# Eight written-out expert steps and a job table made on TensorE and ScalarE, in a four-layer transformer kernel

## The chip, the cores and the metric

The kernel runs on one core of one Trainium2 chip. The metric is the time of one execution on the device in microseconds, the median of three runs. The profile is of one further execution.

## The reference, cut to what matters

The program is two blocks of two layers each, over 256 tokens of width 1024. The first block has attention layers with dense feed-forward parts. Its second layer (layer 1 of the kernel) is a sparse attention whose input product also yields 48 gate columns, and which compresses keys and values with two small weights, `cmp_k_w1` and `cmp_v_w1`. The second block has two layers with a mixture of 32 experts, two experts for each token:

```
experts = grp[:, None] * EXPERTS_PER_GROUP + top_local          # 256 tokens x 2
def expert_block(args):
    xb, e = args
    return (jax.nn.silu(xb @ w_gate[e]) * (xb @ w_up[e])) @ w_down[e]
```

Each expert has a gate and an up weight of 1024x512 and a down weight of 512x1024, in float32: 6 MB for an expert. Which experts get tokens is known only when the router has run. An expert without tokens adds nothing to the output.

## The kernel before, in words

Everything is one program with an instruction stream written for each engine. SyncE (SP) issues nearly all weight loads, in the order in which they are written, each after a wait for the buffer that it overwrites.

**The expert stage.** There are two, one for each layer of the second block. A job is up to 64 slots (`W`) of one expert. After the router, TensorE counts the tokens of each expert. `wm` is the number of jobs of each expert, and expert 0 gets one at least. From these come three results in PSUM bank 3, which VectorE turns into the table `tab`: the expert of each job, the first slot of each job, and `more`, the number of loop rounds. VectorE writes `tab` with three small instructions (L2498, L2499, L2501) between the selection matrix `sel` of token tile 0 and that of tile 1. SP, TensorE, ScalarE and VectorE read registers from `tab`. TensorE runs three dummy products, `spin(3)` (L1673), between the table's products and the gather (L1723) that brings the tokens into slots.

Each job loads six pieces of 1 MB: two of gate, two of up, two of down. Job 0 is always expert 0, and its pieces are loaded before the table is there. TensorE's step `j` makes the gate and up products of job `j` (L1757), transposes (L1766, L1776), and the down products of job `j-1` (L1787). `used` counts the pieces that TensorE has done with.

**Where the pieces go.** `raw` has six places of 1 MB. `spare` has six more, which share their memory with `parts`, the split weights of the other stages. `FIXED` = 6 jobs are handled by code that is written out: jobs 0, 2 and 4 (`IN_PARTS`) go to `spare`, jobs 1, 3 and 5 to `raw`, so up to twelve pieces can be on the way or waiting. From job 6 on, all pieces go to the six places of `raw`. Steps 1 to 5 are written out, the steps after them are a loop over `more` rounds, and the last step and the end are written out again. In the loop the gate piece of the next job waits until TensorE has used the gate piece of this job in the same place. That is in `home_free`:

```
return at(j, 6, q - 7)
```

**Weights elsewhere.** In the other stages a weight is split: ScalarE rounds a piece to its high part (L801) and VectorE subtracts to get the low part (L1941), into one of three places of `parts` (`split_to`). TensorE's products use both parts.

**The gates of layer 1.** The last group of layer 1's input product has 48 columns (`n == 48`). TensorE makes it transposed, ScalarE copies it to `gate_t` (L854), TensorE turns it back (L1613), ScalarE and VectorE each write one token tile of the gates (L859, L1986), and then TensorE goes on with the position products (L1618). The products with the compression windows (L1608) come before and after that, first with `cmp_k_w1`, then with `cmp_v_w1`. Both engines split `cmp_v_w1` ahead of their part in the gates. ScalarE also squares the keys here, which VectorE sums for head norms (L1993).

Of the kernel before, what the change touches and what calls it, by code (L numbers as in the profile page):

```python
# [23 lines left out]
ALU = mybir.AluOpType  # L24
ACT = mybir.ActivationFunctionType
# [23 lines left out]
SPL = 3  # L49
HALF = 2048  # L50
JOBS = NE + NS // W
FIXED = 6
IN_PARTS = (0, 2, 4)
EPS = 1e-6
OFF = -1.0e30
BIG = 3.0e38
# [16 lines left out]
def build(nc, A, out):  # L73
    ctx = ExitStack()
    with ctx:
# [321 lines left out]
        def job_home(l, j, q):  # L397

            if isinstance(j, int) and j <= FIXED:
                job, i = piece(j, q)  # L400
                if job in IN_PARTS:
                    part = (SPL0[2 * l + 1] + i // 2) % SPL
                    return spare[:, 2 * part + i % 2, :], arrived[2 * l][i], 16 * (LOADS0[l][i] + job // 2 + 1)
                if job < FIXED - 1 or j < FIXED:
                    place = (RAW0[2 * l + 1] + i) % RAW
                    return raw[:, place, :], arrived[2 * l + 1][place], 16 * ((job + 1) // 2)
            place = (RAW0[2 * l + 1] + q - 2) % RAW
            return raw[:, place, :], arrived[2 * l + 1][place], at(j, 16, -48 if q < 2 else -32)

        def consumed(job, i):  # L410

# [4 lines left out]
        def home_free(j, q):  # L416

            if isinstance(j, int) and j <= FIXED:
                job, i = piece(j, q)
                if job in IN_PARTS or job == 3 or (job == 5 and i < 4):  # L420
                    return consumed(job - 2, i)
                if job == 5:
                    return consumed(5, i - 2)
                return consumed(3, 4 + i) if i < 2 else consumed(5, i - 2)
            return at(j, 6, q - 7)

        SHAPES = [(4, DE), (4, DE), (2, D)]
# [203 lines left out]
        def _(sp):  # L631
# [33 lines left out]
            for l in range(2):  # L665
                seg = 2 * l
                for i in range(len(stream[seg])):
                    if l == 0 and i == 2:
                        load_x(1, x2_loaded)
                    if l == 0 and i == RAW:  # L670
                        for dst, src in PARS[1:NPAR0] + [(cst[:, P:], A["consts"][:, P:]), (oneh, A["onehot"]), (tmask, A["row_masks"]), (relb[:], A["rel_bias"])]:
                            sp.dma_start(dst, src).then_inc(par_loaded, 16)
                    load(seg, i)
                def gate_up_of(j, e):
                    for q, m, hf in gate_up(j):
                        load_job(l, j, e, q, m, hf)

                def down_of(j, e, last=False):
                    for hf in range(2):
                        load_job(l, j, e, down_at(last) + hf, 2, hf)  # L680

                sp.wait_ge(lo_done[2 * l], len(stream[2 * l]))
                gate_up_of(0, 0)
                down_of(1, 0)
                sp.wait_ge(tab_done, l + 1)
                more = sp.value_load(tab[0:1, 2 * JOBS:2 * JOBS + 1], min_val=NS // W - FIXED - 1, max_val=JOBS - FIXED - 1)
                e = expert(1)
                gate_up_of(1, e)
                down_of(2, e)
                for j in range(2, FIXED + 1):  # L690
                    if j > 2:
                        before = e
                    e = expert(j)
                    gate_up_of(j, e)
                    if j > 2:
                        down_of(j, before)
                with sp.Fori(0, more) as j:
                    e, before = expert(at((j, 1), 1, 0)), expert(at((j, 1), 1, -1))
                    gate_up_of((j, 1), e)
                    down_of((j, 1), before)  # L700
                end = (more, 1)
                down_of(end, expert(at(end, 1, -1)), last=True)
# [82 lines left out]
        def _(act):  # L785
# [59 lines left out]
            def evac_proj(layer, hi):  # L845
                seg = SEG[layer]
                for g in range(PJ_AT[layer], hi):
                    pieces, n, dst = PJ[g]
                    if layer == 1 and g == PJ_AT[1] + 4:
                        compress_in()  # L850
                    split_to(seg, pieces[-1][0] + 3)
                    if n == 48:
                        act.wait_ge(used[seg], pieces[-1][0] + 1)
                        nc.scalar.activation(gate_t, pb[2][0:n, 0:S], ACT.Copy).then_inc(win_a, 1)  # L854
                    act.wait_ge(pj_ready, g + 1)
                    act.wait_ge(rstd_done, ROOT_AT[("norm", N_PROJ[layer])])
                    d = qkv_t(0)[:, dst:dst + n] if layer < 2 else qkv2[:, 0, dst:dst + n]
                    x = pb[2][:, S:S + n] if n == 48 else pb[(2 * g) % 4][:, 0:n]
                    nc.scalar.activation(d, x, ACT.Copy, scale=rstd(N_PROJ[layer], 0)).then_inc(pj_a, 1)  # L859
                    if layer < 2 and g - PJ_AT[layer] in HEADS_AT[layer]:  # L860
                        if layer and g == PJ_AT[1] + 4:
                            split_to(0, CMPW[0] + 1)
                        head_squares(layer, HEADS_AT[layer].index(g - PJ_AT[layer]), g + 1)
# [182 lines left out]
            def moe(l):  # L1046
# [11 lines left out]
                nc.scalar.activation(rt[:, 112:120], rt[:, 112:120], ACT.Exp).then_inc(rt_e, 1)  # L1058
                act.wait_ge(rt_x, 2 * l + 2)
                nc.scalar.activation(rt[:, 364:366], rt[:, 364:366], ACT.Exp).then_inc(rt_e, 1)  # L1060
                for k in range(0, KC, 2):
                    act.wait_ge(ga_ready, KC * l + k + 1)
                    if k == 4:
                        more = act.value_load(tab[0:1, 2 * JOBS:2 * JOBS + 1], min_val=NS // W - FIXED - 1, max_val=JOBS - FIXED - 1)
                    nc.scalar.activation(xsT[:, k, 0:NS], gather_bank(k)[:], ACT.Copy,
                                         scale=gperm[:, l, k:k + 1]).then_inc(xsT_a, 1)
                    if k % 4 == 2:
# [142 lines left out]
        def _(pe):  # L1210
# [464 lines left out]
            def moe(l):  # L1675
# [25 lines left out]
                mm(pos, cm, view(tri[0:NE, :], 0, [[0, 2], [1, NE]]), start=False, stop=True)  # L1701
                mm(pb[3][0:NE, 0:1], tri[0:NE, 0:NE], cm[:, 0:1], start=True, stop=True)
                pe.wait_ge(cnt_done, 2 * l + 2)
                mm(pb[3][0:1, 128:129], wm, ones[0:NE, 0:1], start=True, stop=True)
                mm(pb[3][0:NE, 1:2], tri[0:NE, 0:NE], wm, start=True, stop=True)
                mm(pb[3][0:NE, 2:3], tri[0:NE, 0:NE], wm, start=True, stop=False)
                mm(pb[3][0:NE, 2:3], ident[0:NE, 0:NE], wm, start=False, stop=True).then_inc(pos_ready, 1)
                pe.wait_ge(job_cols, l + 1)
                ja, jo, jv = jobs_work()
                mm(pb[3][0:1, 0:JOBS], ones[0:NE, 0:1], ja, start=True, stop=True)  # L1710
                mm(pb[3][0:1, 64:64 + JOBS], jv, jo, start=True, stop=True).then_inc(job_ready, 1)
                spin(3)
                for group in range(2):
                    for t in range(NT):
                        for i in range(2):
# [25 lines left out]
                    ins.then_inc(gct_ready, 1)  # L1741

                seg = 2 * l + 1
                more = pe.value_load(tab[0:1, 2 * JOBS:2 * JOBS + 1], min_val=NS // W - FIXED - 1, max_val=JOBS - FIXED - 1)

                def landed(j, q, shape):

# [155 lines left out]
        def _(dve):  # L1903
# [57 lines left out]
            def evac_proj(layer, hi):  # L1961
                seg = SEG[layer]
                for g in range(PJ_AT[layer], hi):
# [4 lines left out]
                        head_norms(0, 1)  # L1968
                    if layer == 1 and g == PJ_AT[1] + 4:
                        compress_in()  # L1970
                    split_to(seg, pieces[-1][0] + 3)
                    for part in range((1, 2, 0, 0)[layer]):
                        if g - PJ_AT[layer] == HEADS_AT[layer][part] + 1:
                            head_sums(layer, part)
# [9 lines left out]
                    d = qkv_t(1)[:, dst:dst + n] if layer < 2 else qkv2[:, 1, dst:dst + n]  # L1984
                    x = pb[3][:, S:S + n] if n == 48 else pb[(2 * g + 1) % 4][:, 0:n]
                    v.tensor_scalar(d, x, rstd(N_PROJ[layer], 1), None, ALU.mult).then_inc(pj_v, 1)  # L1986

            def head_sums(layer, part):
                nh = 16 if layer == 0 or part == 0 else 8
# [416 lines left out]
            def route(l):  # L2406
# [56 lines left out]
                cm, wm = rt[0:NE, 512:640], rt[0:NE, 640:641]  # L2463
                v.tensor_copy(cm, pb[1][0:NE, 0:P]).then_inc(cnt_done, 1)
                dve.wait_ge(cnt_done, 2 * l + 1)
                link(v.scalar_tensor_tensor(wm, cm[:, 0:1], 0.0, ident[0:NE, 0:1], ALU.is_gt, ALU.max))
                for i in range(1, S // W):
                    ins = v.scalar_tensor_tensor(wm, cm[:, 0:1], float(i * W), wm, ALU.is_gt, ALU.add)
                    if i < S // W - 1:
# [23 lines left out]
                sl = [slots[:, 0:2], slots[:, 2:4]]  # L2493
                i512 = cst[:, C_I512:C_I512 + NS]
                for t in range(NT):
                    if t:
                        dve.wait_ge(job_ready, l + 1)
                        link(v.tensor_scalar(tab[0:1, 0:JOBS], pb[3][0:1, 0:JOBS], float(NE - 1), None, ALU.min))  # L2498
                        link(v.scalar_tensor_tensor(tab[0:1, JOBS:2 * JOBS], cst[0:1, C_I512:C_I512 + JOBS], float(W),  # L2499
                                                    pb[3][0:1, 64:64 + JOBS], ALU.mult, ALU.add))  # L2500
                        v.tensor_scalar(tab[0:1, 2 * JOBS:2 * JOBS + 1], pb[3][0:1, 128:129], -1.0 - FIXED, None, ALU.add).then_inc(tab_done, 1)  # L2501
                    link(v.tensor_scalar(sel[:, t, :], i512, sl[0][:, t:t + 1], None, ALU.is_equal))
                    v.scalar_tensor_tensor(sel[:, t, :], i512, sl[1][:, t:t + 1], sel[:, t, :].bitcast(F32), ALU.is_equal, ALU.add)\
                        .then_inc(sel_done, 1)
# [11 lines left out]
            def moe(l):  # L2516
# [3 lines left out]
                for k in range(1, KC, 2):  # L2520
# [2 lines left out]
                        .then_inc(xsT_v, 1)  # L2523
                    if k % 4 == 3:
                        gate_rows(k // 4)
                more = dve.value_load(tab[0:1, 2 * JOBS:2 * JOBS + 1], min_val=NS // W - FIXED - 1, max_val=JOBS - FIXED - 1)
                dve.sem_inc(yadd_done[l], 1)
                dve.wait_ge(xsT_a, 5 * (l + 1))
                dve.wait_ge(xsT_v, 5 * (l + 1))
# [189 lines left out]
```

## Time and profile before

| | before |
|---|---|
| median of 3 runs | 1934.6 us (1932.69 to 1934.68) |
| profiled execution, its own time | 1932.56 us |
| its span | 1930.7 us |
| TensorE busy | 1831.7 us, 95% |
| VectorE, ScalarE busy | 863.2 us, 763.3 us |
| DMA | 549.12 MB, mean 284 GB/s |

The span is from the first to the last recorded instruction; 1.9 us of the execution lie around it. TensorE is busy in the records nearly all the time, but its ends are modelled, so a busy share near 100% does not say that it sets the pace. The two expert stages reach from about 830 to 1339 us and from about 1425 to 1922 us.

### The profile page before, as it was taken

To read this page: it belongs to the slowest core of one execution; us is meant where nothing else is said; L and a number is where in the kernel's file an instruction comes from. 1 tells how busy PE (TensorE), PEld (TensorE's weight loads), DVE (VectorE), ACT (ScalarE), POOL (GpSimd) and SP (SyncE) were. 2 spreads that over 40 slices of the span, in tenths; PEclk is the share of its full clock that TensorE was granted. 3 is DMA by queue.
4 is the path that set the end of the run, shared out by engine and by line. 5 is a ranking of instruction groups with operands and counts; after the bars stand their busy time and mean duration, and the time that the engine had idled before them with its cause. 6 is when DMAs were issued, how large, how long until landed. Compare 5 with 4: busy or idle time off the path is not lost.

```text
span 1930.7 us, 28685 instructions
## 1 busy us (share of the span) xinstructions
PE 1831.7 (95%) x10231; PEld 1163.9 (60%) x10231; DVE 863.2 (45%) x1647; ACT 763.3 (40%) x1394; POOL 77.3 (4%) x98
## 2 busy tenths in 40 slices
PE   8999999998999999999999999999999999999997
PEld 6779998875799988874333333335975333333334
DVE  4766556568765566872211111114784111111113
ACT  5554334546543345523332332334532332332333
POOL 3300000120000000010000000000010000000000
PEclk9999999998999999999999999999999999999999
DMA  9545554550355545149999999999338999999995
GB/s 319 207 142 197 189 182 155 183 175 34 118 177 196 177 162 186 45 195 422 394 423 422 422 422 422 422 422 360 133 131 341 418 414 422 422 422 422 422 422 241
DMA packets 154621, 549.12 MB, mean 284 GB/s; under 512 B 10702, under 2 KB 70440, under 8 KB 106152
## 3 DMA queue, kind: packets, MB, share of 16 engines
q1 hardware_dynamic: 151128, 539.52, 71.7%
q0 software_dynamic: 3088, 8.10, 1.3%
q8 instruction: 57, 0.93, 0.2%
q10 hardware_dynamic: 320, 0.34, 0.1%
q14 instruction: 28, 0.23, 0.0%
HBM read 546.81 MB, written 1.11 MB: 284 GB/s over the span
## 4 chain that ended last, share of the span: by engine, by line
PE 60%; DMA 29%; DVE 7%; ACT 2%; issue 1%; POOL 1%; SPq 0%; POOLq 0%; DVEq 0%; ACTq 0%
DMA raw<-in_w_expert_down 28%; PE pb L1228 27%; PE pb L1787 8%; PE pb L1757 8%; PE pb L1523 6%; PE pb L1766 1%; PE pb L1357 1%; PE pb L1457 1%; PE pb L1776 1%; PE pb L1380 1%; POOL rms L781 1%; PE pb L1334 1%; PE pb L1723 1%; DVE parts L1941 1%; PE pb L1240 1%
## 5 line engine op out<-in xcount | busy, mean ns | idle before, releaser
L1757 PE MATMUL pb<-raw,xw 128*64 128x512 f32 x1824 | 439.4, 606 | 0.9
L1941 DVE TENSOR_TENSOR parts<-raw,parts 128x2048 fp32r<-128x2048 f32 (+1 forms) x138 | 307.2, 2231 | 112.7 <-ACT parts L801 109.6
L801 ACT ACTIVATE parts<-raw 128x2048 fp32r<-128x2048 f32 (+1 forms) x138 | 256.5, 1867 | 210.8 <-PE pb L1228 154.3
L1228 PE MATMUL pb<-xT,parts 128*128 128x256 f32 (+1 forms) x2712 | 333.3, 283 | 0.0
L1228 PEld LDWEIGHTS pb<-xT,parts 128*128 128x128 f32 (+1 forms) x2712 | 329.2, 191 | 4.7 <-issue 2.9
L2536 DVE TENSOR_TENSOR qk<-qk,pb 128x256 f32<-128x256 f32 x126 | 53.0, 421 | 611.0 <-ACT qk L1087 610.9
L1228 PE MATMUL pb<-parts,xT 128*128 128x512 f32 (+1 forms) x1200 | 273.4, 386 | 2.6 <-DVE xT L1952 1.5
L1787 PE MATMUL pb<-raw,qk 128*64 128x512 f32 x912 | 217.6, 601 | 46.3 <-DMA raw<-in_w_expert_down 46.3
L1228 PEld LDWEIGHTS pb<-parts,xT 128*128 128x128 f32 x1200 | 218.8, 190 | 49.1 <-issue 4.0
L1757 PEld LDWEIGHTS pb<-raw,xw 128*64 128x64 f32 x1824 | 112.5, 136 | 201.2 <-issue 149.2
L1787 PEld LDWEIGHTS pb<-raw,qk 128*64 128x64 f32 x912 | 61.1, 136 | 196.7 <-issue 138.6
L1082 ACT ACTIVATE qk<-pb 128x512 f32<-128x512 f32 x126 | 74.9, 594 | 182.7 <-PE pb L1757 182.7
L1099 ACT ACTIVATE qk<-pb 128x512 f32<-128x512 f32 x126 | 68.4, 595 | 180.7 <-PE pb L1787 180.7
L1766 PEld LDWEIGHTS pb<-cst,qk 128*128 128x128 f32 x504 | 69.9, 208 | 98.8 <-issue 98.1
L1523 PE MATMUL pb<-parts,hidT 128*128 128x512 f32 x528 | 124.3, 391 | 3.1 <-DVE hidT L2173 3.1
L1523 PEld LDWEIGHTS pb<-parts,hidT 128*128 128x128 f32 x528 | 97.7, 188 | 23.3 <-DVE hidT L2173 3.9
L1087 ACT ACTIVATE qk<-pb 128x256 f32<-128x256 f32 x126 | 48.8, 387 | 123.0 <-PE pb L1766 122.8
L2554 DVE TENSOR_TENSOR work<-work,pb 128x256 f32 x126 | 52.9, 421 | 93.8 <-ACT work L1106 93.1
L1766 PE MATMUL pb<-cst,qk 128*128 128x128 f32 x504 | 93.3, 308 | 0.5 <-DVE rms L2564 0.5
L1106 ACT ACTIVATE work<-pb 128x256 f32 x126 | 48.4, 387 | 114.1 <-PE pb L1776 111.2
L1776 PEld LDWEIGHTS pb<-cst,qk 128*128 128x128 f32 x504 | 54.3, 141 | 48.1 <-issue 47.9
L1776 PE MATMUL pb<-cst,qk 128*128 128x128 f32 x504 | 68.8, 280 | 0.0
(320 smaller groups left out, 1466.3 us busy)
## 6 DMA issues: line engine op xcount, KB each, us to landing
raw<-in_w_expert_gate SPq DMA_DIRECT2D x114, 1024.0 KB, 12.6
raw<-in_w_expert_up SPq DMA_DIRECT2D x114, 1024.0 KB, 12.4
raw<-in_w_expert_down SPq DMA_DIRECT2D x114, 1024.0 KB, 12.7
raw<-in_w_ffn_gate SPq DMA_DIRECT2D x22, 1024.0 KB, 5.1
raw<-in_w_ffn_up SPq DMA_DIRECT2D x22, 1024.0 KB, 5.2
raw<-in_w_ffn_down SPq DMA_DIRECT2D x22, 1024.0 KB, 5.0
raw<-in_w_in SPq DMA_DIRECT2D x16, 1024.0 KB, 5.2
spare<-in_w_expert_gate SPq DMA_DIRECT2D x12, 1024.0 KB, 10.8
```

The source lines that it names most:

```text
L801: nc.scalar.activation(parts[:, (SPL0[seg] + k) % SPL, 0, 0:kk * nn], raw[:, place, 0:kk * nn], ACT.Copy).then_inc(hi_done[seg], 1)
L1082: nc.scalar.activation(dst, pb[bank][:], ACT.Copy).then_inc(done[l], 1)
L1099: nc.scalar.activation(ys[:, 512 * c:512 * (c + 1)], pb[4 + c][:], ACT.Copy).then_inc(ys_done[l], 1)
L1228: ins = mm(out_ap, b if flip else a, a if flip else b, start=first and n == 0, stop=last and n == 2)
L1523: ins = mm(pb[2 * c + t][:], hidT[:, j, i, P * t:P * (t + 1)], w[p][:, j, 512 * c:512 * (c + 1)], start=(q == 1 and j == 0 and n == 0), st ...
L1757: ins = mm(pb[m][rows, :], xw[:, 4 * hf + k, :], w[:, k, :], start=(hf == 0 and k < 2), stop=(hf == 1 and k >= 2))
L1766: ins = nc.tensor.transpose(pb[2 + m][:, P * q:P * (q + 1)], view(src, 256 * (q // 2) + q % 2, [[2, P]]), ident)
L1776: ins = nc.tensor.transpose(pb[6 + b][:, P * q:P * (q + 1)], ys[:, 512 * b + P * q:512 * b + P * (q + 1)], ident)
L1787: ins = mm(pb[4 + c][W * k:W * (k + 1), :], ehj[:, 2 * hf + k, :], w[:, k, 512 * c:512 * (c + 1)], start=(hf == 0), stop=(hf == 1))
L1941: v.tensor_tensor(two[:, 1, :], raw[:, place, 0:kk * nn], two[:, 0, :].bitcast(F32), ALU.subtract)\
L2536: v.tensor_tensor(d, d, pb[2 + m][:].rearrange("p (k i s) -> p k i s", k=4, i=2)[:, :, 1, :], ALU.add)\
L2554: v.tensor_tensor(d, d, pb[6 + b][:].rearrange("p (k i s) -> p k i s", k=4, i=2)[:, :, 1, :], ALU.add)\
```

## The change

- `FIXED` goes from 6 to 8 and job 6 joins the jobs in `spare`. Seven steps (1 to 7) are written out in place of five, and the move to six places comes at job 8.
- The least number of jobs must now be above `FIXED` + 1, so each of the first ten experts (`FORCED`) gets one job at least, in place of expert 0 alone.
- TensorE makes all three results complete: it adds 64 for each job number to the first slots, and subtracts 9 from the number of jobs. These products with constants stand ahead of `pos_ready`. The product that needed to come late is last. One ScalarE copy of 81 values writes `tab`. VectorE's three instructions go, TensorE waits for the table behind `spin(3)`.
- In layer 1, ScalarE copies the gates to `gate_t` ahead of its split of `cmp_v_w1`, and VectorE writes its gates ahead of its part of that split.

```
-FIXED = 6
-IN_PARTS = (0, 2, 4)
+FIXED = 8
+IN_PARTS = (0, 2, 4, 6)
+FORCED = 10
...
-                if job in IN_PARTS or job == 3 or (job == 5 and i < 4):
+                last = FIXED - 1
+                if job < last or (job == last and i < 4):
                     return consumed(job - 2, i)
-                if job == 5:
-                    return consumed(5, i - 2)
-                return consumed(3, 4 + i) if i < 2 else consumed(5, i - 2)
+                if job == last:
+                    return consumed(last, i - 2)
+                return consumed(last - 2, 4 + i) if i < 2 else consumed(last, i - 2)
...
-                    split_to(seg, pieces[-1][0] + 3)
                     if n == 48:
                         act.wait_ge(used[seg], pieces[-1][0] + 1)
                         nc.scalar.activation(gate_t, pb[2][0:n, 0:S], ACT.Copy).then_inc(win_a, 1)
+                    split_to(seg, pieces[-1][0] + 3)
                     act.wait_ge(pj_ready, g + 1)
...
+                act.wait_ge(job_ready, l + 1)
+                nc.scalar.activation(tab[0:1, :], pb[3][0:1, 0:2 * JOBS + 1], ACT.Copy).then_inc(tab_done, 1)
...
-                mm(pb[3][0:1, 128:129], wm, ones[0:NE, 0:1], start=True, stop=True)
...
-                mm(pb[3][0:NE, 2:3], ident[0:NE, 0:NE], wm, start=False, stop=True).then_inc(pos_ready, 1)
+                mm(pb[3][0:NE, 2:3], ident[0:NE, 0:NE], wm, start=False, stop=True)
+                ij = cst[0:1, C_I512:C_I512 + JOBS]
+                left = pb[3][0:1, 2 * JOBS:2 * JOBS + 1]
+                mm(left, wm, ones[0:NE, 0:1], start=True, stop=False)
+                mm(left, cst[0:1, C_I512 + 2 * (FIXED + 1):C_I512 + 2 * (FIXED + 1) + 1], mhalf[0:1, 0:1], start=False, stop=True)
+                mm(pb[3][0:1, JOBS:2 * JOBS], cst[0:1, C_I512 + W:C_I512 + W + 1], ij, start=True, stop=False).then_inc(pos_ready, 1)
                 pe.wait_ge(job_cols, l + 1)
                 ja, jo, jv = jobs_work()
-                mm(pb[3][0:1, 0:JOBS], ones[0:NE, 0:1], ja, start=True, stop=True)
-                mm(pb[3][0:1, 64:64 + JOBS], jv, jo, start=True, stop=True).then_inc(job_ready, 1)
+                mm(pb[3][0:1, JOBS:2 * JOBS], jv, jo, start=False, stop=True)
+                mm(pb[3][0:1, 0:JOBS], ones[0:NE, 0:1], ja, start=True, stop=True).then_inc(job_ready, 1)
                 spin(3)
+                pe.wait_ge(tab_done, l + 1)
...
-                    split_to(seg, pieces[-1][0] + 3)
+                    if n > 48:
+                        split_to(seg, pieces[-1][0] + 3)
...
                     v.tensor_scalar(d, x, rstd(N_PROJ[layer], 1), None, ALU.mult).then_inc(pj_v, 1)
+                    split_to(seg, pieces[-1][0] + 3)
...
-                link(v.scalar_tensor_tensor(wm, cm[:, 0:1], 0.0, ident[0:NE, 0:1], ALU.is_gt, ALU.max))
+                link(v.scalar_tensor_tensor(wm, cm[:, 0:1], 0.0, tri[0:NE, FORCED:FORCED + 1], ALU.is_gt, ALU.max))
...
-                    if t:
-                        dve.wait_ge(job_ready, l + 1)
-                        link(v.tensor_scalar(tab[0:1, 0:JOBS], pb[3][0:1, 0:JOBS], float(NE - 1), None, ALU.min))
-                        link(v.scalar_tensor_tensor(tab[0:1, JOBS:2 * JOBS], cst[0:1, C_I512:C_I512 + JOBS], float(W),
-                                                    pb[3][0:1, 64:64 + JOBS], ALU.mult, ALU.add))
-                        v.tensor_scalar(tab[0:1, 2 * JOBS:2 * JOBS + 1], pb[3][0:1, 128:129], -1.0 - FIXED, None, ALU.add).then_inc(tab_done, 1)
```

## Rows read from the trace of the kernel before

**Rows 1.** The page, the chain that ended last, shares by line.
```profile
DMA raw<-in_w_expert_down 28%; PE pb L1228 27%; PE pb L1787 8%; PE pb L1757 8%; PE pb L1523 6%; PE pb L1766 1%; PE pb L1357 1%; PE pb L1457 1%; PE pb L1776 1%; PE pb L1380 1%; POOL rms L781 1%; PE pb L1334 1%; PE pb L1723 1%; DVE parts L1941 1%; PE pb L1240 1%
```

**Rows 2.** Windows: stretch, length, busy time of engines, clock, DMA share, GB/s.
```profile
930.00:965.00 35.00, 35.00 (x174) 14.01 (x172) 7.33 (x18) 12.39 (x28) 0.00 (x0) 1.00 0.98 383
965.00:1300.00 335.00, 312.31 (x1457) 113.25 (x1454) 54.97 (x136) 103.14 (x227) 0.00 (x0) 1.00 1.01 422
1540.00:1555.00 15.00, 15.00 (x76) 6.19 (x76) 3.08 (x8) 5.23 (x12) 0.00 (x0) 1.00 0.97 381
```

**Rows 3.** Timeline of SP's queue, first expert stage: start, length, issue.
```profile
946.90 2.88 SPq L660 DMA_DIRECT2D raw<-in_w_expert_gate  x2
...
1014.83 2.87 SPq L660 DMA_DIRECT2D raw<-in_w_expert_gate  x2
...
1029.74 2.87 SPq L660 DMA_DIRECT2D raw<-in_w_expert_gate  x2
```

**Rows 4.** The chain in order of time, first expert stage.
```profile
904.77 0.68 PE pb L1766 x4
...
917.90 0.68 PE pb L1766 x4
...
957.30 0.68 PE pb L1766 x4
...
970.44 0.68 PE pb L1766 x4
...
1308.47 1.94 PE pb L1787 x8
```

**Rows 5.** Timeline around the job table, first expert stage.
```profile
848.51 0.21 ACT L1058 ACTIVATE qk<-qk 128x8 f32<-128x8 f32 x1
...
854.57 0.20 PE L1707 MATMUL pb<-qk,cst 32*32 32x1 f32 x2
...
855.24 0.15 DVE L2485 COPY qk<-pb 32x3 f32<-32x3 f32 x1
...
856.15 0.33 PE L1711 MATMUL pb<-qk 32*1 32x40 f32 x2
...
856.41 2.93 PE L1673 MATMUL pb<-cst,ones 128*128 128x256 f32 x6
...
858.18 0.14 DVE L2501 TENSOR_SCALAR tab<-pb 1x1 int32<-1x1 f32 x1
...
859.89 0.87 SPq L660 DMA_DIRECT2D raw<-in_w_expert_gate  x2
```

**Rows 6.** Timeline of the gates of layer 1.
```profile
416.48 1.90 ACT L801 ACTIVATE parts<-raw 128x2048 fp32r<-128x2048 f32 x1
...
417.13 2.05 PE L1608 MATMUL pb<-parts,windows 128*120 128x256 f32 x16
418.28 0.36 ACT L854 ACTIVATE work<-pb 48x256 f32<-48x256 f32 x1
418.41 2.29 DVE L1941 TENSOR_TENSOR parts<-raw,parts 128x2048 fp32r<-128x2048 f32 x1 [3.08 <-ACT parts L801]
...
419.11 0.32 PE L1613 MATMUL pb<-cst,work 48*128 48x48 f32 x2
...
420.62 1.27 DVE L1993 TENSOR_REDUCE rms<-xs 128x8 f32<-128x512 f32 x2
...
421.81 0.26 DVE L1986 TENSOR_SCALAR qkv<-pb,rms 128x48 f32<-128x48 f32 x1
...
422.21 3.57 PE L1618 MATMUL pb<-parts,hidT 128*2 128x256 f32 x16 [2.79 <-DVE qkv L1986]
...
425.58 3.19 PE L1608 MATMUL pb<-parts,windows 128*120 128x256 f32 x16
...
428.61 1.98 PE L1618 MATMUL pb<-parts,hidT 128*2 128x256 f32 x16
```

**Rows 7.** Windows of 1 us in the same place, columns as in rows 2.
```profile
422.00:423.00 1.00, 0.79 (x4) 0.48 (x5) 1.00 (x2) 0.38 (x2) 1.00 (x1) 0.50 0.81 243
```

More of the change, by code:

```diff
@@ L407, in job_home @@
             place = (RAW0[2 * l + 1] + q - 2) % RAW
-            return raw[:, place, :], arrived[2 * l + 1][place], at(j, 16, -48 if q < 2 else -32)
+            return raw[:, place, :], arrived[2 * l + 1][place], at(j, 16, -8 * FIXED + (0 if q < 2 else 16))
         def consumed(job, i):
@@ L685, in _ @@
                 sp.wait_ge(tab_done, l + 1)
-                more = sp.value_load(tab[0:1, 2 * JOBS:2 * JOBS + 1], min_val=NS // W - FIXED - 1, max_val=JOBS - FIXED - 1)
+                more = sp.value_load(tab[0:1, 2 * JOBS:2 * JOBS + 1], min_val=FORCED - FIXED - 1, max_val=JOBS - FIXED - 1)
                 e = expert(1)
@@ L1063, in moe @@
                     if k == 4:
-                        more = act.value_load(tab[0:1, 2 * JOBS:2 * JOBS + 1], min_val=NS // W - FIXED - 1, max_val=JOBS - FIXED - 1)
+                        act.wait_ge(tab_done, l + 1)
+                        more = act.value_load(tab[0:1, 2 * JOBS:2 * JOBS + 1], min_val=FORCED - FIXED - 1, max_val=JOBS - FIXED - 1)
                     nc.scalar.activation(xsT[:, k, 0:NS], gather_bank(k)[:], ACT.Copy,
@@ L1743, in moe @@
                 seg = 2 * l + 1
-                more = pe.value_load(tab[0:1, 2 * JOBS:2 * JOBS + 1], min_val=NS // W - FIXED - 1, max_val=JOBS - FIXED - 1)
+                more = pe.value_load(tab[0:1, 2 * JOBS:2 * JOBS + 1], min_val=FORCED - FIXED - 1, max_val=JOBS - FIXED - 1)
                 def landed(j, q, shape):
@@ L2525, in moe @@
                         gate_rows(k // 4)
-                more = dve.value_load(tab[0:1, 2 * JOBS:2 * JOBS + 1], min_val=NS // W - FIXED - 1, max_val=JOBS - FIXED - 1)
+                dve.wait_ge(tab_done, l + 1)
+                more = dve.value_load(tab[0:1, 2 * JOBS:2 * JOBS + 1], min_val=FORCED - FIXED - 1, max_val=JOBS - FIXED - 1)
                 dve.sem_inc(yadd_done[l], 1)
```

## The prediction

> **What bounds the kernel now.** I read the shares of the chain first. One line stands out: the loads of expert weights hold 28% of the chain [rows 1], so in the expert stages the transfers set the pace, though TensorE shows as busy. Then I cut these stages into windows: after 965 us the loads run at 422 GB/s to the end of the stage [rows 2]. A look at the pace tells more. SP's gate issues come 14.91 us apart in the later rounds, 1014.83 and 1029.74 [rows 3]; six pieces of 1.0486 MB at 422 GB/s are 14.91 us too. TensorE alone is quicker: where it does not wait, its step takes 13.13 us (904.77 to 917.90, written out) and 13.14 us (957.30 to 970.44, in the loop) [rows 4]. So TensorE starts behind the loads, gains 1.8 us on them in each step, catches them between 970 and 1015 us and follows them from there. The last wait for a load ends at 1308.47 [rows 4]; what is left of the stage is TensorE's.
>
> So a microsecond won in the stream of loads before 1308 is won for the layer. The stream has two holes. One is before the table: nothing but job 0 can be loaded until SP has its registers, at 859.89 [rows 5]. The other is where twelve places become six: between 930 and 965 us the rate is 383 in place of 422 [rows 2], a loss of 35 x (1 - 383/422) = 3.2 us. In the second stage it is 381 for 15 us, 1.5 us. The loss is a wait for TensorE: the gate piece of job 7 was issued at 946.90 [rows 3], when TensorE had used that of job 6.
>
> The rest of the kernel is TensorE with VectorE between, as the other lines of the chain say; in it I looked only at the gates of layer 1.
>
> **Part 1, the switch to six places two jobs later.** From the switch on, the order of loads hangs on TensorE's steps, 13.13 us each, and the transfers behind it need 14.91 us for a job. If the switch comes two jobs later while the loads have no hole before it, two jobs more have been loaded in the time in which TensorE did them: at most 2 x (14.91 - 13.13) = 3.6 us for each stage. But loads can't win more than their holes. Alone, the edit can win min(3.6, 3.2) = 3.2 us in the first stage and 1.5 us in the second.
>
> In the second stage TensorE's start stands nearer to the table's time, so its hole is smaller; that is what the 1.5 shows.
>
> I walked the places by hand to see that no other wait takes over: job 6 in `spare` waits for job 4's pieces, which TensorE uses in step 4 (from 917.90 on [rows 4]), so its gate goes out near 921 and not at 929; job 7 waits for job 5; job 8's first gate piece waits for the down of job 5, done at the end of step 6 (which starts at 917.90 + 2 x 13.13 = 944.2) at about 956, when some three pieces are still queued. Down pieces keep their order.
>
> Written-out steps themselves are worth nothing here: 13.13 against 13.14 us [rows 4]. By the Trainium skill, "Advanced Engine Details and Errata", Control Flow Timing, a compare-and-branch is about 108 ns and a plain one 51 ns. If that lay on the path, four rounds fewer would give 4 x 0.16 = 0.6 us more. The rows contradict it for TensorE, and the sum leaves it out.
>
> More code means more instruction loads beside a saturated stream. The steps that are written out now keep 13.13 us under the same load, so I take nothing.
>
> **Part 2, the table.** What is removed: VectorE's three instructions that end at 858.32. What they waited for, the product L1711, ends at 856.48 [rows 5]; VectorE was busy with `sel` in between. New: one ScalarE copy of 1x81 from PSUM. ScalarE is idle there. Its nearest rows are 0.21 us (128x8) [rows 5] and 0.36 us (48x256 from PSUM) [rows 6]; it has 81 elements a row, so I take 0.28, plus 0.05 for the semaphore. The table is there at 856.8 in place of 858.3: 1.5 us sooner, bounds 1.4 and 1.6. From there to SP's first issue are 1.6 us as before.
>
> Two of the products ahead of `pos_ready` are new. Each costs between nothing and what L1711 takes, 0.33 us for 40 columns. L1707 ends at 854.77 and VectorE comes only at 855.24 [rows 5]: 0.47 us of cover. With about 0.35 needed it is hidden; in the worst case 0.2 us comes out of the 1.5. TensorE's new wait stands behind `spin(3)`, which ends at 859.34 [rows 5], 2.5 us after the table. So the gather, and with it TensorE's first expert product, doesn't move. `sel` of tile 1 is 0.5 us sooner, which nobody waits for.
>
> That matters for the sum: if TensorE does not start sooner, loads that start sooner only lead it by more. In the old layout this is lost again at the switch. With part 1 the two together win, for each stage, min(3.6, hole + 1.5): 3.6 us in the first (3.2 + 1.5 = 4.7 is more than enough) and 3.0 us in the second (1.5 + 1.5). Together **6.6 us**. Bounds: the table's 1.4 and the switch at nothing give 0 (it is eaten by the old hole); both stages at the cap give 7.2.
>
> **Part 3, ten experts forced.** A forced expert without tokens costs a whole job, 14.91 us. I counted the tokens of each expert by the reference's router for these inputs: among the first ten the fewest are 5 in the first stage and 4 in the second. The one expert without tokens is number 21, in the second. So no job is added: 32 and 31 before and after.
>
> **Part 4, the gates of layer 1.** TensorE is idle from 419.43, the end of L1613, to 422.21 [rows 6]. It waits for VectorE's gates (L1986, 421.81), which stand behind the split (418.41 to 420.70) and the sums L1993 (1.27 us). After the change VectorE does the sums when ScalarE's squares are there, which is when ScalarE starts its split at 416.48: they are done at 417.8. ScalarE copies `gate_t` (0.36 us) when TensorE has made it, which it has about when L1608 starts at 417.13 [rows 6]; so `gate_t` is there near 417.7, ahead of the turn at 419.11. VectorE writes its gates at 419.5 to 419.75. ScalarE's split takes 1.90 us behind `gate_t`, to 419.6, and its gates 0.30 more, to about 420.0. TensorE goes on at 420.0 in place of 422.2: 2.2 us sooner.
>
> What is late next is `cmp_v_w1`. Its low part takes VectorE 2.29 us from 419.8, to 422.1. TensorE's position products end at 422.0 at full clock (1.98 us as in the row at 428.61 [rows 6]) or 423.6 at half. So the second window products start at 422.1 or 423.6 in place of 425.8.
>
> The clock: in the window at 422 it is 0.50, which is 1.2 GHz, with TensorE idle for 2 us before [rows 7]. The same 16 products take 3.57 us there and 1.98 us later [rows 6]. With an idle time of 0.6 us in place of 2.8 I expect 2.4 GHz throughout. Then the stage ends at 422.1 + 2.05 + 1.98 = 426.1 in place of 430.6: 4.4 us. VectorE then has a second split of 2.29 us and the head norms ahead of its next answer to TensorE, so I take a little less, **4.1 us**. With the clock low as now, 2.2 us. The Trainium skill, "TensorE: Matmul & The Clock Gate", The HAM clock gate, says that the gate looks at activity on a free-running scale, so that a fall isn't bound to one place; by it the low clock could stay even with less idle time. That is the second rival.
>
> No load is late here and the chain to the next stages is TensorE's and VectorE's, so the gain passes on.
>
> **Sum.** 6.6 + 4.1 = 10.7 us. Against the profiled execution's own 1932.56 us that is 1921.9. The median of the runs is 2.0 above that execution, the lowest run 0.1 above it: against the median it is 1923.9. I take 1923.2 between them.
>
> **Rivals.**
> - *The loads win nothing.* The twelve places lose the same at job 8 as now at job 6, or SP's order has a wait that I missed. For it: the early table only adds lead. Against it: the lead shrinks by 1.8 us a step. Only part 4 is left: 1934.6 - 4.1 = 1930.5. If half of the loads' gain comes, 1927.2.
> - *The clock stays low at the gates.* 6.6 + 2.2: 1925.1 on the same scale.
> - *Slower: a forced job.* If one of the first ten experts had no tokens in one stage, the loads would grow by 14.91 us: 1923.2 + 14.9 = 1938.1. One such expert is enough to decide. The counts speak against it.
> - *The gates bring nothing*, because a split that is later starves the next piece: 1934.6 - 6.6 = 1928.0.
>
> **How the numbers follow.** Forecast 60%; clock low 18%; loads half or nothing 13%, of which 5% nothing; gates nothing 6%; a forced job or something of its size 3%. A change of 0.2% is 3.9 us, about what a measurement can tell from none. All cases but the last and the worst of "loads nothing" win more: faster 90%, same 7%, slower 3%. The range goes from both stages at the cap, 4.4 us at the gates, and TensorE's gather up to 1 us quicker in a stage, on the lower scale (1932.6 - 13 = 1919.5) to the half gain of the loads and the gates nothing, about 1928.
>
> **What would show it.** The rate stays at 420 to 422 GB/s from the table on, with no dip near 930 or near 957, and none near 1540. SP issues a gate pair near 921. The first issue after the table comes near 858.3 when TensorE's `spin` is at 856.4 (all about 4 us sooner in absolute time). TensorE's wait for L1986 is under 0.7 us and the clock there is 1.00. It would be wrong if the copy to `tab` took over 1 us, if the dip reappears two steps later, if there are more than 63 jobs, or if VectorE's later split shows as a new wait of L1608.

## The result, and the profile after

The changed kernel takes 1922.62 us (median of 5 runs, 1919.67 to 1923.33), the kernel before 1932.69 us beside it (5 runs). The ratio is 0.9947 (0.9934 to 0.9959): 10.2 us less. The profiled execution took 1919.67 us with a span of 1917.8; it is the shortest of the five.

The page: the span, and the chain by line. The loads' share fell from 28% to 26% [rows 1].
```profile
span 1917.8 us, 28529 instructions
...
PE pb L1233 27%; DMA raw<-in_w_expert_down 26%; PE pb L1767 9%; PE pb L1797 8%; PE pb L1528 6%; PE pb L1776 2%; PE pb L1786 1%; PE pb L1362 1%; PE pb L1462 1%; PE pb L1385 1%; POOL rms L783 1%; PE pb L1339 1%; DVE parts L1951 1%; PE pb L1733 1%; PE pb L1245 1%
```

Windows of the changed kernel, columns as in rows 2. The 383 and 381 GB/s of before [rows 2] are gone. What is left is a small dip in the first stage, now 25 us long and later: 25 x (1 - 411/422) = 0.65 us there. By windows of 5 us, which reach to 978 us, and against 421 GB/s it is 1.1 us, where before it was 3.2. The second stage has no dip, at the old place or behind it.
```profile
920.00:950.00 30.00, 30.00 (x148) 11.53 (x146) 4.89 (x12) 10.31 (x22) 0.00 (x0) 1.00 1.01 421
950.00:975.00 25.00, 25.00 (x124) 9.87 (x122) 4.89 (x12) 8.73 (x20) 0.00 (x0) 1.00 1.01 411
975.00:1300.00 325.00, 303.41 (x1418) 110.21 (x1414) 53.80 (x132) 100.23 (x221) 0.00 (x0) 1.00 1.01 421
...
1530.00:1560.00 30.00, 30.00 (x150) 12.31 (x152) 6.07 (x15) 10.21 (x24) 0.00 (x0) 1.00 1.01 421
1560.00:1870.00 310.00, 289.59 (x1352) 105.11 (x1348) 52.22 (x128) 96.17 (x212) 0.00 (x0) 1.00 1.01 422
```

SP's queue in the first stage. Job 6's gate goes to `spare` at 913.99. The stage begins 6.6 us sooner than before, so this is 920.6 on the scale of before. The long pause of SP is now ahead of job 8, and the gate issue that hangs on TensorE is the one at 966.53 in place of 946.90 [rows 3].
```profile
913.99 2.88 SPq L662 DMA_DIRECT2D spare<-in_w_expert_gate  x2
...
949.13 2.05 SPq L662 DMA_DIRECT2D raw<-in_w_expert_gate  x2
...
966.53 2.88 SPq L662 DMA_DIRECT2D raw<-in_w_expert_gate  x2
```

The timeline around the table, which answers to [rows 5]. The last new product (L1716) ends at 848.47, before VectorE comes at 848.71. ScalarE's copy takes 0.23 us and is done 0.34 us after the dummy products begin. From their start to SP's issue it is 1.89 us; before it was 859.89 - 856.41 = 3.48.
```profile
848.18 0.29 PE L1716 MATMUL pb<-cst 1*1 1x40 f32 x2
...
848.71 0.15 DVE L2497 COPY qk<-pb 32x3 f32<-32x3 f32 x1
...
849.62 0.33 PE L1720 MATMUL pb<-qk,ones 32*1 32x40 f32 x2
...
849.88 2.93 PE L1678 MATMUL pb<-cst,ones 128*128 128x256 f32 x6
849.99 0.23 ACT L1064 ACTIVATE tab<-pb 1x81 int32<-1x81 f32 x1 [4.05 <-PE pb L1720]
...
851.77 0.87 SPq L662 DMA_DIRECT2D raw<-in_w_expert_gate  x2
```

The timeline of the gates, which answers to [rows 6]. VectorE sums first, waits for the turn, writes its gates at 419.75, and TensorE goes on at 420.16, 0.45 us late in place of 2.79. The position products take 2.00 us where they took 3.57.
```profile
416.37 1.28 DVE L2005 TENSOR_REDUCE rms<-xs 128x8 f32<-128x512 f32 x2 [0.75 <-ACT xs L879]
...
417.61 0.38 ACT L855 ACTIVATE work<-pb 48x256 f32<-48x256 f32 x1 [0.76 <-PE pb L1233]
...
419.39 0.32 PE L1618 MATMUL pb<-cst,work 48*128 48x48 f32 x2
...
419.75 0.27 DVE L1997 TENSOR_SCALAR qkv<-pb,rms 128x48 f32<-128x48 f32 x1 [2.10 <-PE pb L1618]
...
420.16 2.00 PE L1623 MATMUL pb<-parts,hidT 128*2 128x256 f32 x16 [0.45 <-ACT qkv L861]
...
422.27 2.14 PE L1613 MATMUL pb<-parts,windows 128*120 128x256 f32 x16
...
424.25 2.03 PE L1623 MATMUL pb<-parts,hidT 128*2 128x256 f32 x16
```

The window of 1 us there, columns as in rows 2: the granted clock is 1.00, where it was 0.50 [rows 7].
```profile
421.00:422.00 1.00, 1.00 (x11) 0.64 (x8) 1.00 (x1) 1.00 (x3) 0.01 (x1) 1.00 0.00 0
```

**Where the time went.** From the start of the 48 columns' product to the first product behind the windows (L1625 before, L1630 after) it is 16.05 us before and 11.45 after. An expert stage, from SP's first expert issue to the end of the last product into tokens, took 513.13 and 495.52 us and takes 509.57 and 492.82: 3.6 and 2.7 less. That is 10.9 of the 12.9 us between the two spans. The rest, 2.0 us, is not the change's: 2.3 us won behind the gates, less 0.3 lost ahead of them. The way from those first products to SP's first expert issue takes 399.1 us before and 396.8 after, and the difference lies between 438 and 456 us, at the start of layer 1's attention, where the change does nothing: the clock was at 0.50 for some 14 us in the execution of before and for 7 in that of after.

### The profile page after: what moved, and what is told of

The parts are those of the page before. It is cut to its first block, busy times and chain, and to the rows that moved or that the text cites. A ratio compares the mean times of both kernels' runs of the same rounds, so it can differ in the third digit from the quotient of the medians.

```text
span 1917.8 us, 28529 instructions
## 1 busy us (share of the span) xinstructions
PE 1824.4 (95%) x10239; PEld 1160.8 (61%) x10239; DVE 862.5 (45%) x1641; ACT 764.0 (40%) x1396; POOL 75.3 (4%) x98
## 4 chain that ended last, share of the span: by engine, by line
PE 62%; DMA 27%; DVE 6%; ACT 2%; issue 1%; POOL 1%; SPq 0%; POOLq 0%; DVEq 0%; ACTq 0%
PE pb L1233 27%; DMA raw<-in_w_expert_down 26%; PE pb L1767 9%; PE pb L1797 8%; PE pb L1528 6%; PE pb L1776 2%; PE pb L1786 1%; PE pb L1362 1%; PE pb L1462 1%; PE pb L1385 1%; POOL rms L783 1%; PE pb L1339 1%; DVE parts L1951 1%; PE pb L1733 1%; PE pb L1245 1%
## 5 line engine op out<-in xcount | busy, mean ns | idle before, releaser
L1767 PE MATMUL pb<-raw,xw 128*64 128x512 f32 x1760 | 423.6, 606 | 0.9
L1797 PE MATMUL pb<-raw,qk 128*64 128x512 f32 x880 | 209.6, 601 | 42.3 <-DMA raw<-in_w_expert_down 42.3
```

What stands on the lines that cost most here:

```text
L1767: ins = mm(pb[m][rows, :], xw[:, 4 * hf + k, :], w[:, k, :], start=(hf == 0 and k < 2), stop=(hf == 1 and k >= 2))
L1797: ins = mm(pb[4 + c][W * k:W * (k + 1), :], ehj[:, 2 * hf + k, :], w[:, k, 512 * c:512 * (c + 1)], start=(hf == 0), stop=(hf == 1))
```

## The experiments

The times of all runs are compared with executions of the kernel before that ran beside them. A stage's length is taken as just described. Three times are counted from SP's first expert issue: the first issue behind the table, the start of step 2, and the end. Each row is one profiled execution. e1, e2, e3, e5, e9, e10 and e12 have the rest of the kernel before; e4, e6, e7, e8 and e11 are made from the changed kernel, and all of these but e4 have the new order of the gates.

| run | first stage: issue, step 2, end | second stage: issue, step 2, end |
|---|---|---|
| before | 30.38, 62.05, 513.13 | 30.16, 59.38, 495.52 |
| changed | 28.82, 61.98, 509.57 | 28.56, 59.44, 492.82 |
| e1 gates | 30.38, 61.69, 512.83 | 30.16, 62.32, 498.31 |
| e2 FIXED 8 | 30.39, 61.79, 510.65 | 30.12, 62.01, 494.60 |
| e3 table | 28.81, 62.23, 513.61 | 28.46, 59.45, 495.37 |
| e4 both | 28.81, 61.91, 510.33 | 28.55, 62.12, 494.30 |
| e5 dummies | 30.40, 58.32, 510.54 | 30.18, 58.32, 494.85 |
| e6 ten, old table | 30.41, 62.01, 510.70 | 30.13, 62.04, 494.71 |
| e7 ten | 28.82, 61.94, 509.24 | 28.41, 59.45, 493.04 |
| e8 ten, SP | 28.26, 61.98, 509.13 | 27.86, 60.98, 492.74 |
| e9 ScalarE's half of gates | 30.39, 61.95, 513.75 | 30.16, 62.16, 497.00 |
| e10 VectorE's half of gates | 30.40, 61.85, 513.10 | 30.15, 59.28, 495.15 |
| e11 22 forced | 28.80, 62.15, 510.54 | 28.54, 59.29, 508.00 |
| e12 table, dummies | 28.71, 58.26, 509.97 | 28.47, 59.87, 495.58 |

**The four parts, alone and together.** e1 has the gates' new order on the kernel before.

> The kernel before with the reordered gates of layer 1 alone. My theory: TensorE's wait for the gates of VectorE shrinks from 2.8 to about 0.5 us and the clock there stays at 1.00, so the stretch from the gates' product to the products behind them is 4.6 us shorter, as in the changed kernel; the median falls by 4 to 5 us. Both expert stages keep their lengths of before (479.0 and 462.3 us from SP's first expert issue to the last down product that waits for a load). Rival, the part of the profile's gain that lies behind the gates (2.2 us between 430 and 830 us) comes from this edit too: then the median falls by 6 to 7 us in every execution.

1927.18 us, ratio 0.9981 (0.9971 to 0.9990): 3.7 us less. The stretch at the gates is 11.46 us, as in the changed kernel. In the other executions with the old order (e2, e3, e4, e5, e12) it is 14.8 to 14.9, since the clock fell later in it and came back sooner than in the profile of before. So the edit is worth 3.5 us as a rule and 4.6 against that one profile; 4 to 5 us in the median were expected. The clock fell in this stretch in all seven profiles in which VectorE splits first, and in none of the seven in which it writes its gates first. The rival, that the time behind 430 us comes from this edit too and the median falls by 6 to 7 us, is outside the interval, which ends at 5.6.

Against what I expected, e1's second stage is 2.8 us longer than before. The profiled execution, 1931.55 us, is the longest of e1's twelve. Rows of its timeline and, in the second fence, of that of the kernel before at the same place: the gather (L1723) takes 9.56 us in place of 8.17, and the first products of step 1 (L1757 x8) 3.15 in place of 1.94. The loads were no later.
```profile
1451.07 9.56 PE L1723 MATMUL pb<-hidT,xsp 128*128 128x512 f32 x32
...
1471.28 3.15 PE L1757 MATMUL pb<-raw,xw 128*64 128x512 f32 x8
```
```profile
1454.85 8.17 PE L1723 MATMUL pb<-hidT,xsp 128*128 128x512 f32 x32
...
1473.67 1.94 PE L1757 MATMUL pb<-raw,xw 128*64 128x512 f32 x8
```
The windows over the gather, e1 and then the kernel before, columns as in rows 2: the granted clock is 0.82 and 1.00.
```profile
1452.00:1460.00 8.00, 8.00 (x31) 7.36 (x29) 4.10 (x6) 1.69 (x3) 0.00 (x0) 0.82 0.86 333
```
```profile
1456.00:1464.00 8.00, 8.00 (x36) 7.19 (x37) 5.21 (x9) 2.75 (x5) 0.00 (x0) 1.00 0.91 352
```

e2 has the later switch with the old table:

```
-FIXED = 6
-IN_PARTS = (0, 2, 4)
+FIXED = 8
+IN_PARTS = (0, 2, 4, 6)
+FORCED = 10
...
```

> The kernel before with FIXED = 8, job 6 in spare and the ten forced experts, but the table made by VectorE as before. My theory (the loads win their hole at the switch, at most 3.6 us): the first stage shrinks by 2.5 to 3.2 us, the second by 1.5 to 1.8, and the rate has no dip near 930 us. Rival, the switch two jobs later gives its full 3.6 us whatever the hole: 3.6 in each stage.

1928.21 us, ratio 0.9985 (0.9976 to 0.9994). The first stage is 2.5 us shorter. The second is only 0.9 shorter than before, but its step 2 began at 62.01 and not at 59.38. Against e1, where step 2 began at 62.32, it is 3.7 shorter, and against e9 (62.16) 2.4. What the switch is worth depends on when TensorE starts.

e3 has the table alone, FIXED = 6 (eight experts forced).

> The kernel before with the table made by TensorE and ScalarE alone, FIXED = 6. My theory: SP's first issue after the table comes 1.5 us sooner against TensorE's dummy products, the hole at the switch grows by the same 1.5 us, and the stages keep their lengths within 0.3 us: no gain in time. Rival, the gains are additive: each stage is 1.5 us shorter, 3 us in all.

1931.39 us, ratio 0.9997 (0.9987 to 1.0007): nothing. The issue behind the table comes 1.57 and 1.70 us sooner, the stages keep their lengths (0.5 longer, 0.15 shorter). The window at the switch shows where it went: 367 GB/s in place of 383, so 35 x (1 - 367/422) = 4.6 us are lost in place of 3.2.
```profile
928.00:963.00 35.00, 35.00 (x174) 13.94 (x172) 7.33 (x18) 12.39 (x28) 0.00 (x0) 1.00 0.94 367
```

e4 is the changed kernel with the gates in their old order.

> The changed kernel with the gates of layer 1 in their old order: the later switch and the early table together. My theory: 3.5 us in the first stage and 2.7 to 3.0 in the second, as in the changed kernel, which is more than the sum of the two alone (4.0 to 5.0 and 0). Rival, additive: the sum of the two runs beside this one.

1925.67 us, ratio 0.9972 (0.9961 to 0.9984): 5.4 us less, where e2 and e3 have 2.9 and 0.6 by themselves. The intervals alone don't settle that this is more than the sum. The stages are 2.8 and 1.2 shorter than before, not 3.5 and 2.7. In the second, step 2 began late again, at 62.12. In the first it did not (61.91, changed kernel 61.98), and the code is the same, but the stage is 0.8 us longer: two profiles of the same code can differ by that much.

**What sets the end of a stage.** The rows of before, e1 and e3 showed a rule. With FIXED = 6 a stage ends 436.1 us behind the start of step 2: before 495.52 - 59.38 = 436.14 and 513.13 - 14.91 - 62.05 = 436.17, e1 436.2 and 436.0, e3 436.5 and 435.9 (first and second stage), though the table moved by 1.6 us or the start by 2.9. The later runs show that it holds to about 1 us only: e9 has 436.9 and 434.8, e10 436.3 and 435.9. In e9's second stage TensorE first waits for a load one step later than in e1's, and why is open. The other bound is the loads': 465.3 us behind the first issue in the first stage without its 32nd job (e2), 464.3 in the second (changed kernel). e5 tries it from TensorE's side: only dummy products are added to the kernel before.

```
-                spin(10)
+                spin(14)
...
+                spin(2)
                 pe.wait_ge(job_cols, l + 1)
```

> The kernel before, unchanged but for more dummy products of TensorE in the router part: 14 in place of 10 behind the router's products and 2 more where TensorE waits for VectorE's job columns, so that its clock should not fall before the gather. The table isn't sooner. My theory (with FIXED = 6 the end of a stage hangs on TensorE's start and not on the table): the stage, from SP's first expert issue to the last product into tokens, ends 436.1 us after the start of step 2 (after 14.9 us for the 32nd job are taken off in the first stage), wherever that start is, so a gather 2 to 3 us sooner makes each stage as much shorter, 4 to 5 us in all. Rival, the loads set the end: the stages keep 513.1 and 495.5 us.

1928.18 us, ratio 0.9979 (0.9970 to 0.9988). Step 2 starts at 58.32 in both stages, which would give 509.3 and 494.4; the loads' bound gives 510.6 and 494.5. Measured are 510.54 and 494.85. So I had forgotten my own second bound: 2.6 and 0.7 us were won in the stages of this profile, not 4 to 5. The ratio says 4.1 us less, between 2.3 and 5.8, and executions of the kernel before whose second stage starts late, as e1's did, may be why; that was not tried. But with TensorE that early there is no hole at the switch, with six places as they were:
```profile
929.00:964.00 35.00, 35.00 (x174) 13.98 (x174) 6.92 (x17) 12.00 (x27) 0.00 (x0) 1.00 1.01 421
```

e6 and e7 try the loads' side, on the changed kernel with its gates: FIXED = 10, job 8 in `spare`, twelve forced, with the old table (e6) and the new (e7).

> The changed kernel with FIXED = 10, job 8 in spare too and twelve forced experts (no job is added), but the old table on VectorE. My theory: with ten jobs written out no load ever waits for TensorE, so the end of a stage hangs on the table alone: 465.3 us (first, without its 32nd job) and 464.3 us (second) after the first issue behind the table, which is 510.6 and 494.5 us from the first expert issue. Rival, TensorE's start still counts: the stages scatter with it by up to 3 us.

> The changed kernel with FIXED = 10, job 8 in spare and twelve forced experts. My theory: both stages hang on the table alone, 1.55 us sooner than with the old table: 509.1 and 492.9 us; 0.5 us less than the changed kernel in the first, nothing in the second where TensorE starts early, up to 1.5 us where it starts late. Rival, the early table is lost as with FIXED = 6: the same lengths as with the old table.

e6: 1922.99 us, ratio 0.9959 (0.9945 to 0.9974); e7: 1921.04 us, 0.9947 (0.9933 to 0.9961). Expected were 510.6 and 494.5, then 509.1 and 492.9; measured 510.70 and 494.71, then 509.24 and 493.04. Now the early table is worth 1.5 and 1.7 us, where in e3 it was worth nothing. In e6 the second stage's step 2 began at 62.04 and cost nothing. In e7 the dip is gone from the first stage, at the old place and at that of the changed kernel, 145 to 155 us behind the first expert issue. The last fence has the changed kernel's windows at this second place. The stage is 0.3 us shorter than the changed kernel's (509.24 against 509.57), and 1.1 and 1.3 shorter than in e4 and e11, which have the changed kernel's code there.
```profile
924.00:959.00 35.00, 35.00 (x174) 14.01 (x172) 7.34 (x18) 12.39 (x28) 0.00 (x0) 1.00 1.01 422
...
969.11:974.11 5.00, 5.00 (x30) 2.02 (x28) 1.52 (x4) 1.26 (x3) 0.00 (x0) 1.00 1.01 421
974.11:979.11 5.00, 5.00 (x26) 1.82 (x24) 0.00 (x0) 2.24 (x5) 0.00 (x0) 1.00 1.01 418
```
```profile
967.95:972.95 5.00, 5.00 (x30) 2.02 (x28) 1.55 (x4) 1.26 (x3) 0.00 (x0) 1.00 1.00 393
972.95:977.95 5.00, 5.00 (x26) 1.85 (x24) 0.00 (x0) 2.20 (x4) 0.00 (x0) 1.00 0.98 365
```

e8 adds to e7 that SP reads `more` last:

```
-                more = sp.value_load(tab[0:1, 2 * JOBS:2 * JOBS + 1], min_val=FORCED - FIXED - 1, max_val=JOBS - FIXED - 1)
                 e = expert(1)
                 gate_up_of(1, e)
                 down_of(2, e)
+                more = sp.value_load(tab[0:1, 2 * JOBS:2 * JOBS + 1], min_val=FORCED - FIXED - 1, max_val=JOBS - FIXED - 1)
```

> As the one before with ten jobs, and SP reads the number of loop rounds only after it has issued job 1, so that its first issue behind the table comes about 0.4 to 0.6 us sooner. My theory: the stages shrink by as much, to about 508.6 and 492.4 us. Rival: the loads of the down weights land at the same time, since the table isn't what they wait for.

1920.96 us, ratio 0.9940 (0.9926 to 0.9954). The first issue is 0.56 us sooner in both stages, the ends only 0.1 and 0.3, where as much as the issue was expected. It is the lowest ratio of all, but neither e7 nor e8 can be told from the changed kernel by its time. Where the other 0.3 to 0.4 us of each stage went I did not find.

**The gates, half by half.** e9 moves only ScalarE's copy to `gate_t`, e10 only VectorE's split behind its gates.

```
+                    if n > 48:
+                        split_to(seg, pieces[-1][0] + 3)
...
                     v.tensor_scalar(d, x, rstd(N_PROJ[layer], 1), None, ALU.mult).then_inc(pj_v, 1)
+                    split_to(seg, pieces[-1][0] + 3)
```

> The kernel before, with ScalarE's half of the gates edit alone: gate_t is copied ahead of ScalarE's split, VectorE still does its part of the split and the sums ahead of its gates. My theory: it is VectorE's order that made TensorE wait; here its split starts about 1.2 us later, behind ScalarE's, so TensorE waits about 4 us for the gates in place of 2.8, and the stretch is longer than before. Rival, the gates' copy to gate_t is what was late: the wait shrinks.

> The kernel before, with VectorE's half alone: its gates ahead of its part of the split, ScalarE in its old order. My theory: all of the gain, TensorE waits about 0.5 us, the second window products start within 0.3 us of where they start with both halves (4.9 us behind the end of the turn's product's start, at the full clock). Rival, both halves are needed: the wait shrinks only in part.

One execution each: 1937.29 and 1926.30 us (before: 1931.9). The row of e9's waits, then that of e10's timeline:
```profile
PE pb L1618 <- DVE qkv L1986: 3.9, 1, 3.9
```
```profile
418.72 1.98 PE L1618 MATMUL pb<-parts,hidT 128*2 128x256 f32 x16 [0.45 <-ACT qkv L859]
```
ScalarE's half alone makes TensorE wait 3.9 us, 1.1 more than before. VectorE's half alone leaves 0.45 us, and its stretch is 424.64 - 413.23 = 11.41 us, as with both. e9's stretch is 17.02 us. All of this part's gain is VectorE's order: one execution for each half, but both waits are far apart.

**A forced job.** e11 sets FORCED = 22.

> The changed kernel with 22 experts forced in place of ten, which takes in the one expert without tokens in the second stage. My theory: a job more there and none in the first stage: the second stage is 14.9 us longer (507.7 us from the first expert issue), the first keeps 509.6, and the program is slower than before by 4 to 5 us. Rival, an empty job costs less than a load's 14.9 us since it has no tokens.

One execution: 1937.86 us, 6.0 above the kernel before. The second stage is 508.00 us long in place of 492.82, so a job without tokens costs 15.2 us. In the first stage, where nothing is added, it is 1.0 us longer than in the changed kernel: step 2 began 0.2 later, and by windows of 5 us the dip at the switch cost 2.0 us in place of 1.1.

**Both bounds in one run.** e12 is e3 with e5's dummy products.

> The kernel before with the early table and FIXED = 6, and the dummy products that keep TensorE's clock up. My theory: a stage is as long as the later of two ends asks: 436.1 us behind step 2, and 465.3 (first) or 464.3 us (second) behind the first issue after the table, with 14.9 us more in the first stage. With step 2 at 58.3 and the issue at 28.8 that is 509.3 and 494.4 us, so the early table is worth 1.2 and 0.4 us here though it was worth nothing without the dummy products. Rival: it is worth nothing with FIXED = 6 anyway.

1927.61 us, ratio 0.9978 (0.9969 to 0.9987). In the first stage the table is worth 0.6 us over e5 (509.97 against 510.54), where 1.2 was expected; that is less than two profiles of the same code differ by. The dip at the switch, gone in e5, is back: by windows of 5 us it costs 1.1 us.
```profile
937.67:942.67 5.00, 5.00 (x28) 2.01 (x24) 0.88 (x3) 2.05 (x5) 0.00 (x0) 1.00 0.98 408
942.67:947.67 5.00, 5.00 (x30) 2.02 (x28) 1.57 (x4) 1.26 (x3) 0.00 (x0) 1.00 0.98 392
947.67:952.67 5.00, 5.00 (x26) 1.87 (x24) 0.00 (x0) 2.19 (x4) 0.00 (x0) 1.00 0.99 367
```
In the second, step 2 began at 59.87 in spite of the dummies, as the clock fell in step 1; the rule gives 436.1 + 59.87 = 496.0, measured 495.58. So that stage says nothing on the table, and the ratio is e5's within the intervals: what the table is worth with FIXED = 6 and an early TensorE stays open.

## Why the prediction was right

It was 1923.2 us for 1922.62 measured; 10.7 us less in the sum, 10.2 by the ratio. The direction, the holes and the gates were right as mechanisms. That the number is so close has some luck in it. The kernel before was put at 1933.9 us, between a median and a profile, and ran at 1932.69 beside the changed one; and the stages' terms were met in one profile and not in others, as follows.

- **The loads bound and its two holes** were right. e3 shows the part that mattered: an early table alone is lost at the switch. e6 and e7 show that it pays when nothing is lost there.
- **min(3.6, hole + 1.5)** gave 3.6 and 3.0; the changed kernel has 3.6 and 2.7, but e4, with the same code in the expert stages, has 2.8 and 1.2, and e11's first stage 2.6. So 6.6 us were met by 6.3 in one profile and by 4.0 in another. The first hole was also priced somewhat high: the rates gave 3.2 us, and the three runs with the old table and no dip there (e2, e5, e6) end at 510.54 to 510.70, 2.4 to 2.6 us sooner than before. And the size of the hole was not a constant of the kernel, as I took it: it follows TensorE's start. With a late start the second stage lost 3.7 us by 5 us windows (e1) in place of 1.4 in the profile of before. So the change can win more in executions with a slow gather (from e1 to e4 the second stage is 4.0 us shorter, from e9 to e4 2.7), and the second stage's 3.0 came from one draw.
- **No dip near 957** was wrong, and by my own sum: a hole of 4.7 with a cap of 3.6 leaves 1.1 us, and 1.1 us is there by the rates. e7 takes it away; its stage is 3.9 us shorter than before, not 4.7.
- **The table**: 1.5 us expected, 1.56 and 1.60 measured; the copy 0.23 us for 0.28. The products ahead of `pos_ready` were covered. TensorE's new wait cost nothing: the gather starts 29.30 us behind the first expert issue, before it was 29.27. It starts 2.0 us behind the table, not 2.5.
- **The forced experts** added no job, and one would have cost 15.2 us (14.91 estimated). This rival's price was right. The rivals were not all priced on one scale: the low clock and the forced job go from 1933.9 us for the kernel before, the others from 1934.6.
- **The gates**: 4.1 us chosen; 4.6 between the profiles, 3.5 against the other executions, 3.7 by e1's ratio. The clock stayed up, so the second rival fell. What I did not see is that ScalarE's half does nothing, and harms alone.
- **Written-out steps** show no worth of their own: where the loads are the bound, a first stage with five of them is as long as one with nine (e5 510.54, e6 510.70).
- The two profiles differ by 2.0 us beyond the three terms, in the attention of layer 1. That is the clock: this way takes 396.8 us with 7 us of low clock, in the new order of the gates (changed kernel, e6) and in the old (e3), and 399.1 us with 14, again in both (e7, before). What decides between them was not tried.

## What to carry to other kernels

When two engines take turns to be late, an edit on one of them is worth only what the other leaves: write down both bounds for the end of the stage and take the later, before and after. A hole in a saturated stream may be caused by the consumer's start far ahead of it, so deeper buffers, an earlier consumer and an earlier producer are three prices for the same hole, not three gains. And before a profile's stretch is taken as a constant, look whether the granted clock in it is the same in a second execution.

## What the runs showed of the hardware

TensorE's clock scatters between executions of the same code. At the start of layer 1's attention it was at 0.50 for some 14 us (before, e4), 10 (e1) and 7 (changed kernel), and for 14 in e7, whose code up to there is the changed kernel's. In the second expert stage the gather took 8.17 us (before) or 9.56 (e1), with FIXED = 6 in both, and e1's stage was 2.8 us longer; in e9, with 9.39 us, it was 1.5 longer. TensorE had idled 1.6 us ahead of the router's counts in before and in e1. The Trainium skill says in "TensorE: Matmul & The Clock Gate", The HAM clock gate, that the gate's view of the activity is free-running; these executions agree in that the same code met the low clock at different places. With FIXED = 10 a late start no longer shows in the stage (e6: step 2 at 62.04, end at 494.71, the loads' bound 494.4).
